# Modulation sums of a two-layer DiT trunk: VectorE folds the accumulators in turned 32x32 blocks, TensorE adds four partition groups with a selector

## The chip, the cores and the metric

The kernel runs on one core of a Trainium2 chip. The metric is device time in microseconds (us) of one execution. Five engines run in parallel, each through its own stream of instructions, and wait for one another by semaphores: TensorE (PE) multiplies 128x128 blocks and writes PSUM banks, VectorE (DVE) and ScalarE (ACT) work on elements, GpSimd (POOL) here mostly issues the DMAs of one weight matrix, SyncE (SP) issues the DMAs of all others.

## The reference, cut to what matters

Two layers of a trunk over 256 latent tokens (`x`) and 256 context tokens (`xc`), with 1024 channels, all in fp32. Each layer is FFN, mixers (attention and a short convolution), FFN, and every one of these is modulated by vectors made from a conditioning vector:

```python
c_act, cc_act = silu(c), silu(c_ctx)                # two vectors of 1024
mod  = (c_act  @ w_ada + b_ada).reshape(B, 9, 1, D) # w_ada: 1024 x 9216 in each layer
modc = (cc_act @ w_ada + b_ada).reshape(9, D)
x  = x  + 0.5 * mod[:, 2] * swiglu(modulate(rmsnorm(x, norm_w[0]), mod[:, 0], mod[:, 1]), ffn1_wi, ffn1_wo)
xc = xc + 0.5 * modc[2]   * swiglu(modulate(rmsnorm(xc, norm_w[0]), modc[0], modc[1]), ffn1_wi, ffn1_wo)
# mixers with mod 3, 4, 5; second FFN with mod 6, 7, 8
```

What the change touches is only `c_act @ w_ada` and `cc_act @ w_ada`: two rows times a 1024 x 1024 block of `w_ada` for each of 18 modulation vectors. All else is what stands beside it.

## The kernel before, in words

**Streamed weights.** Each large product takes 1024x1024-float pieces of weights through a ring of four slots (`raw`, `wH`, `wL`). SP loads `raw`; ACT copies it rounded to `wH` (`hi`, L1071); DVE makes the rest `wL = raw - wH` (`lo`, L1355); PE multiplies three times for every product (`triple`, L585 to L587), with the activations split in the same way. PE signals `w_used` behind each piece; a piece of 24 matmuls of 512 columns is one step of the ring. DVE signals `lo_done`, for which PE waits at the start of a piece. DVE makes the second pair of parts of a group of four pieces for the group that follows, so it is two pieces ahead.

**Modulation vectors.** The first two are made by PE at the very start (`ada_sums`, `ada_turn` with n < 4). The other 16 are spread over the kernel as five batches (`ADA_BATCHES`): 4, 2, 4, 2 and 4 vectors. Batches 0, 2 and 4 ("wi") run beside the first product of FFN 0, 1 and 2; batches 1 and 3 ("wo") beside the second product of FFN 0 and 1. POOL loads a 128x1024 row block of `w_ada` into one of four buffers; DVE multiplies it by a value per partition and adds it to the accumulator `acc` (`ada_tile`, L1399 for the first of eight blocks, L1402 for the other seven), twice, for `c` and for `c_ctx`. After eight blocks `acc[:, v, :]` (128 x 2 x 1024) still has to be summed over the 128 partitions.

**Sum over the partitions.** PE does it (`ada_reduce`, L611 to L619): four matmuls, one for each of the two vectors and two halves, with 4 columns of a one-hot matrix `oneh` as the stationary operand and 512 columns of `acc` moving. Each of the four writes another strip of 32 partitions of PSUM bank 5 (named `scored` in the trace), and the place of the one in `oneh` chooses the row of the vector within the strip. In the "wi" batches this stands in PE's order behind every second group of four pieces (four times in a batch), in the "wo" batches twice at once, in the opening of what follows (`ada_reduce_late`), when the new normed activations are being made. DVE may start the next accumulation in `acc` only when `ada_red` says that PE has read it.

**Rows to columns.** DVE copies bank 5 to `rowS` (`batch_rows`, L1378), PE turns it with four transposes (`ada_turn`, L607) into bank 6 (`turned`), and DVE adds the bias and writes `mod` (`batch_evac`, L1389). Bank 5 is set to zero by DVE before each use. In the "wi" batches PE's turn stands within group 9 of 11, in the "wo" batches within the opening.

**Order.** Each engine's order is written out by hand. PE's order in an FFN with a batch: the opening (pieces 0 to 3), groups 1 to 10, with `ada_reduce` after groups 2, 4, 6 and 8 and the turn inside group 9; then the second product. DVE's order in a group: `lo`, a block, `lo`, a block, two products (`product`, L1579 and L1587), `lo`, a block, `lo`, a block.

Of the kernel before, what the change touches and what calls it, by code (L numbers as in the profile page):

```python
# [7 lines left out]
P = 128  # L8
# [141 lines left out]
def build(nc, x, c, ctx, c_ctx, w_ada, b_ada, norm_w, ffn1_wi, ffn1_wo, w_in, conv_w, sink, w_oa, w_ob, w_out,  # L150
          ffn2_wi, ffn2_wo, final_norm_w, consts, out):
    stack = ExitStack()
    with stack:
# [34 lines left out]
        oneh = sb("oneh", [P, 16])  # L188
        sb("to_row", [P, 95])
        with ExitStack() as r:  # L190
# [5 lines left out]
            with ExitStack() as s:  # L196
                acc2 = s.enter_context(nc.sbuf_tensor("acc2", [P, 2, D], F32))

# [67 lines left out]
        ada_red = sem("ada_red")  # L266
        oneh_set = sem("oneh_set")
# [311 lines left out]
        def _(pe):  # L579
# [22 lines left out]
            def ada_turn(n):  # L602

                pe.wait_ge(row_out, n + 1)
                wait(pe, ada_out, n if n < QUARTERS else 2 * n - QUARTERS)
                for q in range(2 if n < QUARTERS else 4):
# [12 lines left out]

            def ada_reduce_late(b):  # L620

                pe.wait_ge(x_ready, x_count(b, DC - 1, 1))
                for u in range(2):
                    ada_reduce(acc[:] if u == 0 else acc2[:], 2 * DC * (ada_before(b) + u + 1), 3 - u, start=(u == 0))

            def opening(n0, v, ts, mids={}, between=None, ahead={}):
# [51 lines left out]
                for kk in (4, 6):  # L678
                    for j in (2, 3):
# [7 lines left out]
                        if kk == 6 and j == 2 and v in (1, 3):  # L687
                            ada_turn(QUARTERS + v)
# [146 lines left out]
            def ffn(f, v):  # L835
# [5 lines left out]
                def first_group():  # L841

                    if n0 > 0:
                        opening(n0, v, (t, t), second_norm(v) if halves(t) == 2 else {},
                                (lambda: ada_reduce_late(v)) if v == 3 else None)
# [5 lines left out]
                def group(i, turn=None):  # L851
# [3 lines left out]
                    for j in range(4):  # L855
# [3 lines left out]
                        if turn is not None and j == 1:  # L859
                            ada_turn(turn)  # L860
# [99 lines left out]
            def mixers(l):  # L960
# [4 lines left out]
                        (lambda: ada_reduce_late(v)) if v == 1 else None)  # L965
# [371 lines left out]
        def _(dve):  # L1337
# [36 lines left out]
            def batch_rows(b):  # L1374

                dve.wait_ge(ada_red, ada_before(b + 1))
                dve.wait_ge(ada_T, QUARTERS + b)
                nc.vector.tensor_copy(rowS[:], ps[5][:]).then_inc(row_out, 1)  # L1378

            def batch_evac(b):  # L1380

                _, _, first, count = ADA_BATCHES[b]
                dve.wait_ge(ada_T, QUARTERS + 1 + b)
                part = ps[6][:].rearrange("p (q v h u) -> p v u h q", q=4, v=2, h=2)
                at = V_BADA + DC * first
                bias = VT[:, at:at + DC * count].rearrange("p (u h q) -> p u h q", u=count, h=2)
                for v in range(2):
                    dst = mod[:, first:first + count, :, v].rearrange("p u (h q) -> p u h q", h=2)
                    tt(dst, part[:, v, 0:count], bias, ALU.add).then_inc(ada_out, 1)  # L1389

            def ada_tile(dst, src, n, reduced):
# [3 lines left out]
                if k == 0:  # L1395
                    wait(dve, ada_red, reduced)
# [475 lines left out]
```

## Time and profile before

| | us |
|---|---|
| median of 3 runs | 1832.9 (1832.73 to 1833.56) |
| profiled execution, span | 1832.8 |
| PE busy | 1818.3 (99%) |
| PE weight loads busy | 1543.2 (84%) |
| DVE busy | 1121.4 (61%) |
| ACT busy | 693.6 (38%) |
| POOL busy | 99.3 (5%) |

The profiled execution's own time is the span of 1832.8 us, 0.1 us from the median of the three timed runs. "Busy" of PE counts from the first to the last cycle of overlapping matmuls: a matmul of 512 columns has a record of 0.39 us, yet the next starts about 0.23 us after it.
### The profile page before, as it was taken

How to read it: one execution, taken by the hardware profiler on the slowest of the kernel's cores; microseconds unless marked ns; L12 is line 12 of the kernel's file. 1: busy time of each engine (PE TensorE's matmuls, PEld its weight loads, DVE VectorE, ACT ScalarE, POOL GpSimd, SP SyncE). 2: the span in 40 equal slices, each digit the busy share in tenths (PEclk: the TensorE clock that was granted, in tenths of full speed). 3: DMA queues.
4: the chain of work that ended last, by engine and by line, in shares of the span. 5: the costliest groups of instructions: out<-in, count | busy, mean ns of one | idle time of the engine just before them, and what ended most of it. 6: DMA issues, size and time to landing. Idle time of an engine off the chain costs nothing.

```text
span 1832.8 us, 26314 instructions
## 1 busy us (share of the span) xinstructions
PE 1818.3 (99%) x10131; PEld 1543.2 (84%) x10131; DVE 1121.4 (61%) x1506; ACT 693.6 (38%) x1093; POOL 99.3 (5%) x174
## 2 busy tenths in 40 slices
PE   9999999999999999999999999999999999999998
PEld 6888888888777789888888888888888888999998
DVE  5877737556554366877737557777422487676554
ACT  3433332244334324433332144333322365556543
POOL 0101001010000001000001010000000100000000
PEclk9999999999999999999999999999999999999999
DMA  9766526423222323666527435565222254546663
GB/s 335 227 189 189 155 92 232 146 70 102 74 78 70 92 80 127 185 191 188 159 92 229 149 115 172 176 196 169 92 94 101 69 150 139 150 143 202 195 195 115
DMA packets 187893, 271.49 MB, mean 148 GB/s; under 512 B 25388, under 2 KB 154908, under 8 KB 187804
## 3 DMA queue, kind: packets, MB, share of 16 engines
q1 hardware_dynamic: 168912, 202.74, 35.8%
q0 software_dynamic: 18432, 67.12, 12.0%
q8 instruction: 64, 1.05, 0.2%
q10 hardware_dynamic: 460, 0.39, 0.1%
q14 instruction: 25, 0.20, 0.0%
HBM read 269.16 MB, written 1.05 MB: 147 GB/s over the span
## 4 chain that ended last, share of the span: by engine, by line
PE 94%; DVE 3%; ACT 2%; issue 1%; DMA 0%; SPq 0%; ACTq 0%; DVEq 0%
PE ps L585 23%; PE ps L586 23%; PE ps L587 23%; PE turned L586 2%; PE turned L587 2%; PE turned L585 2%; PE scored L585 2%; PE scored L586 2%; PE scored L587 2%; PE ps L642 2%; PE ps L644 2%; PE ps L654 2%; PE turned L956 1%; PE turned L939 1%; PE scored L925 1%; PE scored L616 1%
## 5 line engine op out<-in xcount | busy, mean ns | idle before, releaser
L1355 DVE TENSOR_TENSOR wL<-raw,wH 128x1024 fp32r<-128x1024 f32 x364 | 443.3, 1223 | 447.4 <-ACT wH L1071 447.1
L1071 ACT ACTIVATE wH<-raw 128x1024 fp32r<-128x1024 f32 x364 | 383.1, 1057 | 663.8 <-PE ps L587 658.4
L585 PE MATMUL ps<-hH,wH 128*128 128x512 f32 (+1 forms) x1592 | 583.0, 366 | 0.6 <-ACT T L1164 0.6
L586 PE MATMUL ps<-hL,wH 128*128 128x512 f32 (+1 forms) x1592 | 578.5, 363 | 0.0
L587 PE MATMUL ps<-hH,wL 128*128 128x512 f32 (+1 forms) x1592 | 578.4, 363 | 0.0
L585 PEld LDWEIGHTS ps<-hH,wH 128*128 128x128 f32 x1592 | 299.0, 188 | 64.7 <-issue 16.3
L587 PEld LDWEIGHTS ps<-hH,wL 128*128 128x128 f32 x1592 | 298.9, 188 | 48.3
L586 PEld LDWEIGHTS ps<-hL,wH 128*128 128x128 f32 x1592 | 299.0, 188 | 46.5
L585 PE MATMUL ps<-GH,wH 128*128 (+2 forms) x376 | 131.5, 350 | 0.0
L587 PE MATMUL ps<-GH,wL 128*128 (+2 forms) x376 | 131.2, 349 | 0.0
L586 PE MATMUL ps<-GL,wH 128*128 (+2 forms) x376 | 131.2, 349 | 0.0
L1402 DVE SCALAR_TENSOR_TENSOR acc<-adaC,cact,acc 128x1024 f32<-128x1024 f32 x96 | 118.8, 1278 | 0.0
L1183 ACT ACTIVATE T<-ps 128x512 f32<-128x512 f32 (+1 forms) x88 | 43.1, 541 | 154.6 <-PE ps L587 148.9
L1171 ACT ACTIVATE GH<-T 128x512 f32 (+3 forms) x88 | 49.4, 579 | 114.1 <-DVE T L1579 114.1
L585 PEld LDWEIGHTS ps<-GH,wH 128*128 128x128 f32 x376 | 70.8, 188 | 9.5
L586 PEld LDWEIGHTS ps<-GL,wH 128*128 128x128 f32 x376 | 70.8, 188 | 9.3
L587 PEld LDWEIGHTS ps<-GH,wL 128*128 128x128 f32 x376 | 70.7, 188 | 9.3
L560 POOL TENSOR_TENSOR T<-T 128x256 f32<-128x256 f32 x30 | 22.9, 764 | 969.8 <-ACT T L1076 968.9
L1579 DVE TENSOR_TENSOR T<-T 128x512 f32<-128x512 f32 (+1 forms) x88 | 50.8, 619 | 31.2 <-ACT T L1164 31.2
L1402 DVE SCALAR_TENSOR_TENSOR acc<-adaW,cact,acc 128x1024 f32<-128x1024 f32 x56 | 69.3, 1278 | 0.0
L585 PE MATMUL ps<-nearH,wH 128*128 128x256 f32 x240 | 68.8, 287 | 0.0
L642 PE MATMUL ps<-hH,wH 128*128 128x256 f32 (+1 forms) x208 | 65.0, 332 | 2.8 <-ACT hH L1086 2.0
(249 smaller groups left out, 2509.4 us busy)
## 6 DMA issues: line engine op xcount, KB each, us to landing
raw<-in_ffn_wi SPq DMA_DIRECT2D x176, 512.0 KB, 3.9
raw<-in_ffn_wo SPq DMA_DIRECT2D x88, 512.0 KB, 3.4
raw<-in_w_in SPq DMA_DIRECT2D x60, 512.0 KB, 3.9
adaC<-in_w_ada POOLq DMA_DIRECT2D x48, 512.0 KB, 4.4
adaW<-in_w_ada POOLq DMA_DIRECT2D x32, 512.0 KB, 4.3
adaA<-in_w_ada POOLq DMA_DIRECT2D x24, 512.0 KB, 4.0
adaB<-in_w_ada POOLq DMA_DIRECT2D x24, 512.0 KB, 4.6
raw<-in_w_out SPq DMA_DIRECT2D x16, 512.0 KB, 3.3
```

Source lines behind the costliest of these rows:

```text
L585: mm(dst, wa, ra, start=start, stop=False, **kw)
L586: mm(dst, wa, rb, start=False, stop=False, **kw)
L587: return mm(dst, wb, ra, start=False, stop=stop, **kw)
L642: mm(ps[banks(j) + b][:, cols], wH[:, s, w], h_of(v)[0][:, kk, rows], start=(kk == 0 and cols.start == 0), stop=False, skip_group_check=True)
L644: mm(ps[banks(j) + b][:, cols], wL[:, s, w], h_of(v)[0][:, kk, rows], start=False, stop=False, skip_group_check=True)
L654: last = mm(ps[banks(j) + b][:, cols], wH[:, s, weights(j, kk % 4, b)], h_of(v)[1][:, kk, rows], start=False, stop=(kk == DC - 1), skip_gr ...
L1071: av(wH[:, s, :], raw[:, s, :], ACT.Copy).then_inc(hi_done, 1)
L1171: av(dst, T[:, 2 + b, 0:t], ACT.Copy).then_inc(g_hi, 1)
L1183: av(T[:, b, 0:t], ps[b][:, 0:t], ACT.Copy).then_inc(a_out, 1)
L1355: tt(wL[:, s, :], raw[:, s, :], wH[:, s, :].bitcast(F32), ALU.subtract).then_inc(lo_done, 1)
L1402: stt(dst[:, v, :], src, cact[:, v, k:k + 1], dst[:, v, :], ALU.mult, ALU.add).then_inc(acc_step, 1)
L1579: tt(T[:, 2 + b, 0:t], T[:, 2 + b, 0:t], T[:, b, 0:t], ALU.mult).then_inc(g_prod, 1)
```

## The change

The one-hot sums, the copy to rows and the transposes of the five batches go. Instead:

- DVE sums each accumulator itself over blocks (`fold`): one `tensor_reduce` over `acc` seen as 64 blocks of 32 columns, with `apply_transpose`, which turns each 32x32 block on the way in. What comes out is 128 x 64: in each group of 32 partitions, each partition holds the sum over the 32 partitions of its group, for one of every 32 columns. In "wi" batches it stands behind every second group and writes 64 columns of `rowS`; in "wo" batches it stands behind the block j = 8 (the first one of the second vector) and the block j = 15 and writes `late_sums`.
- PE adds the four groups of partitions (`ada_spread_out`): once in a batch, four matmuls with a 128x32 selector `sel` as the stationary operand and 64 (or 32, in "wo") columns of sums with a stride of four floats moving; each writes one strip of 32 partitions of bank 6. It stands where the turn stood in "wi" batches and where the late sums stood in "wo" batches.
- DVE adds the bias from bank 6 (`batch_evac`), with no copy to rows before. `ada_tile` waits for DVE's own `ada_folded` where it waited for PE.
- DVE makes `sel` once from the identity. `oneh` and the clearing of bank 5 between batches go.

```diff
-            def ada_reduce(src, steps, at, start=False):
-                pe.wait_ge(acc_step, steps)
-                for v in range(2):
-                    for h in range(2):
-                        g = 2 * v + h
-                        last = mm(ps[5][32 * g:32 * g + 4, :], oneh[:, at:at + 4],
-                                  src[:, v, h * TOK:(h + 1) * TOK], start=start, stop=True, skip_group_check=True)
-                last.then_inc(ada_red, 1)
-            def ada_reduce_late(b):
+            def ada_spread_out(b):
+                count = ADA_BATCHES[b][3]
+                sums = (rowS[:, 0:2 * D // 32 * count] if ADA_BATCHES[b][1] == "wi" else
+                        late_sums[:].rearrange("p u v c -> p (u v c)"))
+                pe.wait_ge(sel_set, 1)
+                pe.wait_ge(ada_folded, ada_before(b + 1))
+                pe.wait_ge(ada_out, QUARTERS + 2 * b)
+                for r in range(4):
+                    last = mm(ps[6][32 * r:32 * r + 32, 0:2 * DC * count], sel[:],
+                              sums.rearrange("p (n r) -> p n r", r=4)[:, :, r], start=True, stop=True, skip_group_check=True)
+                last.then_inc(ada_spread, 1)
+            def ada_late(b):
                 pe.wait_ge(x_ready, x_count(b, DC - 1, 1))
-                for u in range(2):
-                    ada_reduce(acc[:] if u == 0 else acc2[:], 2 * DC * (ada_before(b) + u + 1), 3 - u, start=(u == 0))
+                ada_spread_out(b)
...
-                        if kk == 6 and j == 2 and v in (1, 3):
-                            ada_turn(QUARTERS + v)
...
-                    pe.wait_ge(oneh_set, 1)
-                    pe.wait_ge(bank5_zero, f + 2)
-                    for p in range(4):
-                        group(2 * p + 1)
-                        group(2 * p + 2)
-                        ada_reduce(acc[:], 2 * DC * (ada_before(b) + p + 1), 3 - p, start=(p == 0))
-                    group(GROUPS - 2, QUARTERS + b)
+                    for i in range(1, GROUPS - 2):
+                        group(i)
+                    group(GROUPS - 2, b)
...
-            def batch_rows(b):
-                dve.wait_ge(ada_red, ada_before(b + 1))
-                dve.wait_ge(ada_T, QUARTERS + b)
-                nc.vector.tensor_copy(rowS[:], ps[5][:]).then_inc(row_out, 1)
...
-                dve.wait_ge(ada_T, QUARTERS + 1 + b)
+                dve.wait_ge(ada_spread, b + 1)
...
+            def fold(src, dst, n):
+                dve.wait_ge(acc_step, 2 * DC * (n + 1))
+                nc.vector.tensor_reduce(dst, src[:].rearrange("p v (c i) -> p (v c) i", i=32), AX_X, ALU.add,
+                                        apply_transpose=True).then_inc(ada_folded, 1)
...
-                    if hf == nh - 1 and m == 5 and v in (1, 3):
-                        batch_rows(v)
...
-                if v in (2, 3):
-                    nc.vector.memset(ps[5][:], 0.0).then_inc(bank5_zero, 1)
...
+                if f == 0:
+                    nc.vector.tensor_reduce(sel[:], ident.rearrange("p (r j) -> p j r", r=4), AX_X, ALU.add
+                                            ).then_inc(sel_set, 1)
...
                         group(2 * u + 2, DC * u + 4)
-                    batch_rows(b)
+                        fold(acc, rowS[:, 2 * D // 32 * u:2 * D // 32 * (u + 1)], ada_before(b) + u)
...
+                        if j in (DC, 2 * DC - 1):
+                            u = j // DC if j > DC else 0
+                            fold(acc2 if u else acc, late_sums[:, u].rearrange("p v c -> p (v c)"), ada_before(b) + u)
```

## Rows read from the trace of the kernel before

**Rows 1.** The page: busy time of the engines, and the chain that ended last.

```profile
PE 1818.3 (99%) x10131; PEld 1543.2 (84%) x10131; DVE 1121.4 (61%) x1506; ACT 693.6 (38%) x1093; POOL 99.3 (5%) x174
...
PE 94%; DVE 3%; ACT 2%; issue 1%; DMA 0%; SPq 0%; ACTq 0%; DVEq 0%
```

**Rows 2.** Timeline of PE, one sum: start, duration, what, count.

```profile
96.65 0.39 PE L587 MATMUL ps<-hH,wL 128*128 128x512 f32 x1
...
98.69 0.39 PE L587 MATMUL ps<-hH,wL 128*128 128x512 f32 x1
99.01 1.04 PE L616 MATMUL scored<-acc,oneh 128*4 128x512 f32 x8
99.98 0.50 PE L585 MATMUL ps<-hH,wH 128*128 128x512 f32 x1
100.32 0.39 PE L586 MATMUL ps<-hL,wH 128*128 128x512 f32 x1
```

**Rows 3.** The chain in order of time (start, duration): sums of "wi" batches.

```profile
99.08 0.97 PE scored L616 x8
143.80 0.97 PE scored L616 x8
...
1247.87 0.97 PE scored L616 x8
1292.63 0.97 PE scored L616 x8
```

**Rows 4.** Timeline of PE around the late sums of batch 1.

```profile
406.94 0.64 PE L654 MATMUL ps<-hL,wH 128*128 128x256 f32 x4
407.51 1.90 PE L616 MATMUL scored<-acc,oneh 128*4 128x512 f32 x16
409.34 0.38 PE L642 MATMUL ps<-hH,wH 128*128 128x256 f32 x1
409.56 0.28 PE L644 MATMUL ps<-hH,wL 128*128 128x256 f32 x1
```

**Rows 5.** Timeline of PE around the turn of batch 0.

```profile
244.99 0.40 PE L587 MATMUL ps<-hH,wL 128*128 128x512 f32 x1
245.22 0.60 PE L607 MATMUL turned<-cst,rowS 128*128 128x128 f32 x4
...
246.82 0.39 PE L587 MATMUL ps<-hH,wL 128*128 128x512 f32 x1
```

**Rows 6.** Timeline of PE around eight narrow records with full weights (mean squares).

```profile
394.93 0.28 PE L587 MATMUL ps<-GH,wL 128*128 128x256 f32 x1
395.05 0.51 PE L803 MATMUL scored<-cst,T 128*128 128x2 f32 x4
395.41 0.59 PE L803 MATMUL scored<-cst,sqT 128*128 128x2 f32 x4
...
396.06 0.28 PE L586 MATMUL ps<-GL,wH 128*128 128x256 f32 x1
```

**Rows 7.** Groups of weight loads by form: busy us, mean ns, idle before.

```profile
L803 PEld LDWEIGHTS scored<-cst,T 128*128 128x128 f32 x16 | 2.1, 192 | 0.0
...
L616 PEld LDWEIGHTS scored<-acc,oneh 128*4 128x4 f32 x128 | 2.0, 85 | 5.8 <-issue 5.5
```

**Rows 8.** Groups of DVE by form: a reduction over 1024 elements.

```profile
L1720 DVE TENSOR_REDUCE stat<-scored 128x2 f32<-128x1024 f32 x16 | 19.6, 1225 | 0.6
```

**Rows 9.** Timeline of DVE where the first fold will stand; idle before in brackets.

```profile
90.47 2.48 DVE L1402 SCALAR_TENSOR_TENSOR acc<-adaC,cact,acc 128x1024 f32<-128x1024 f32 x2
95.74 1.23 DVE L1355 TENSOR_TENSOR wL<-raw,wH 128x1024 fp32r<-128x1024 f32 x1 [2.79 <-ACT wH L1071]
100.19 1.42 DVE L1399 TENSOR_SCALAR acc<-adaA,cact 128x1024 f32<-128x1024 f32 x2 [3.23 <-PE scored L616]
```

**Rows 10.** Busy time in one stretch from sum to sum: length, PE, PEld, DVE, ACT, POOL, PE clock.

```profile
99.00:143.70 44.70, 44.70 (x201) 36.08 (x200) 32.88 (x32) 14.61 (x20) 4.22 (x8) 1.00 0.63 188
```

**Rows 11.** Waits: total us, times, longest.

```profile
DVE acc L1399 <- PE scored L616: 29.1, 9, 3.2
DVE rowS L1378 <- PE scored L616: 21.5, 3, 7.2
```

**Rows 12.** Timeline of DVE in the second product of FFN 0.

```profile
318.85 1.41 DVE L1399 TENSOR_SCALAR acc<-adaW,cact 128x1024 f32<-128x1024 f32 x2
323.15 1.23 DVE L1355 TENSOR_TENSOR wL<-raw,wH 128x1024 fp32r<-128x1024 f32 x1 [2.89 <-ACT wH L1071]
```

**Rows 13.** Timeline of the opening after the late sums: ACT's h parts, then PE.

```profile
414.10 0.51 ACT L1086 ACTIVATE hH<-T,mod 128x256 fp32r<-128x256 f32 x1 [1.41 <-DVE T L1427]
```

**Rows 14.** The same opening, PE's first matmul of chunk 5.

```profile
416.58 0.39 PE L642 MATMUL ps<-hH,wH 128*128 128x512 f32 x1
```

More of the change, by code:

```diff
@@ L186, in build @@
         stat = sb("stat", [P, 6, 4])
-        oneh = sb("oneh", [P, 16])
-        sb("to_row", [P, 95])
+        sel = sb("sel", [P, P // 4])
+        sb("to_row", [P, 79])
         with ExitStack() as r:
@@ L265, in build @@
         acc_step = sem("acc_step")
-        ada_red = sem("ada_red")
-        oneh_set = sem("oneh_set")
+        ada_folded = sem("ada_folded")
+        ada_spread = sem("ada_spread")
+        sel_set = sem("sel_set")
         ada_out = sem("ada_out")
@@ L604, in ada_turn @@
                 pe.wait_ge(row_out, n + 1)
-                wait(pe, ada_out, n if n < QUARTERS else 2 * n - QUARTERS)
-                for q in range(2 if n < QUARTERS else 4):
+                wait(pe, ada_out, n)
+                for q in range(2):
                     last = nc.tensor.transpose(ps[6][:, q * P:(q + 1) * P], rowS[:, q * P:(q + 1) * P], ident)
                 last.then_inc(ada_T, 1)
-            def ada_reduce(src, steps, at, start=False):
-                pe.wait_ge(acc_step, steps)
-                for v in range(2):
-                    for h in range(2):
-                        g = 2 * v + h
-                        last = mm(ps[5][32 * g:32 * g + 4, :], oneh[:, at:at + 4],
-                                  src[:, v, h * TOK:(h + 1) * TOK], start=start, stop=True, skip_group_check=True)
-                last.then_inc(ada_red, 1)
-            def ada_reduce_late(b):
+            def ada_spread_out(b):
[10 more added lines that the diff above has]
+            def ada_late(b):
                 pe.wait_ge(x_ready, x_count(b, DC - 1, 1))
-                for u in range(2):
-                    ada_reduce(acc[:] if u == 0 else acc2[:], 2 * DC * (ada_before(b) + u + 1), 3 - u, start=(u == 0))
+                ada_spread_out(b)
             def opening(n0, v, ts, mids={}, between=None, ahead={}):
@@ L844, in first_group @@
                         opening(n0, v, (t, t), second_norm(v) if halves(t) == 2 else {},
-                                (lambda: ada_reduce_late(v)) if v == 3 else None)
+                                (lambda: ada_late(v)) if v == 3 else None)
                         return
@@ L849, in first_group, with group @@
                             None, {1: lambda: ada_sums(1), 3: lambda: ada_sums(2), 5: lambda: ada_sums(3)})
-                def group(i, turn=None):
+                def group(i, batch=None):
                     pe.wait_ge(a_out, i * 2 + 2 * GROUPS * f)
@@ L858, in group @@
                         columns_piece(n0, j, 2 * (j % 2), j // 2, t, i, span(t))
-                        if turn is not None and j == 1:
-                            ada_turn(turn)
+                        if batch is not None and j == 1:
+                            ada_spread_out(batch)
                 b = ada_batch(f, "wi")
@@ L964, in mixers @@
                 opening(n0, v, (TOK, t), second_norm(v),
-                        (lambda: ada_reduce_late(v)) if v == 1 else None)
+                        (lambda: ada_late(v)) if v == 1 else None)
                 for h in range(4, PROJ_P):
@@ L1372, in ada_evac, with ada_tile @@
                 tt(dst, part[:, :, :, 1, 0:2], dst, ALU.add).then_inc(ada_out, 1)
[L1374 to L1378 removed]
             def batch_evac(b):
                 _, _, first, count = ADA_BATCHES[b]
[L1383 to L1384 removed]
+                dve.wait_ge(ada_spread, b + 1)
+                part = ps[6][:, 0:2 * DC * count].rearrange("p (u v k) -> p v u k", u=count, v=2)
                 at = V_BADA + DC * first
[L1386 removed]
+                bias = VT[:, at:at + DC * count].rearrange("p (u k) -> p u k", u=count)
                 for v in range(2):
[L1388 to L1391 removed]
+                    tt(mod[:, first:first + count, :, v], part[:, v], bias, ALU.add).then_inc(ada_out, 1)
+            def ada_tile(dst, src, n, folded):
                 k = n % DC
@@ L1395, in ada_tile @@
                 if k == 0:
-                    wait(dve, ada_red, reduced)
+                    wait(dve, ada_folded, folded)
                 for v in range(2):
@@ L1829, in _ @@
             nc.vector.memset(ps[5][:], 0.0).then_inc(bank5_zero, 1)
-            mark(nc.vector.memset(oneh[:], 0.0))
-            settle()
-            nc.vector.memset(oneh[:, 3:4], 1.0).then_inc(oneh_set, 1)
             for hf in range(2):
```

2 lines of the change are left out of this document (1 added, 1 removed).

## The prediction

> **What bounds the kernel now.** I read the page first: PE is busy for 1818.3 of 1832.8 us, and 94% of the chain that ended last is PE's [rows 1]. So a PE instruction that goes away is time won, as long as nobody else becomes late; DVE, at 61%, has room on average, and the question is whether it has room where the new work is put. Then I looked for the instructions that go in the chain in order of time: the "wi" sums stand on it, 0.97 us each, three of four shown in pairs 44.7 us apart [rows 3]. To price them I went to PE's timeline around each kind, because matmul records overlap and only the distance between starts is a cost.
>
> **The cadence.** From 96.65 to 98.69 there are nine steps: 2.04 / 9 = 0.2267 us for a matmul of 512 columns [rows 2]. Half width goes at 0.12 us.
>
> **Removed from PE.** (a) *Twelve "wi" sums.* Between the starts of two of them lie eight pieces of 24 matmuls: 143.80 - 99.08 = 44.72 us, and 1292.63 - 1247.87 = 44.76 [rows 3]; 192 x 0.2267 is 43.52. One sum therefore costs 1.20 us, refilling the pipeline included. The direct view agrees: L586 starts at 100.32 where the cadence would have put it at 98.69 + 0.45 = 99.14, so 1.18 [rows 2]. 12 x 1.20 = 14.4 us. (b) *Two pairs of late sums.* The four L654 from 406.94 end their steps at 407.42, the L644 after the next would start at 407.54 and starts at 409.56: 2.02 us [rows 4]. 2 x 2.02 = 4.0. (c) *Five turns.* From 244.99 to 246.82 are six steps, 1.36 us by the cadence, and it took 1.83: 0.47 us [rows 5]. 5 x 0.47 = 2.4. Together 20.8 us, all in PE's order and with PE busy on both sides.
>
> **Added to PE: five spreads.** The trace has no 128x32 stationary operand, so I bound it. One sum costs 1.20, two in a row 2.02: the second, eight records of 512 columns in four strips, costs 0.82, and entering and leaving costs 0.38. The spread is eight records in the same four strips with 64 columns (three batches) or 32 (two): 0.82 x 64 / 512 = 0.10 or 0.05. That gives the lower bound, 0.48 and 0.43 us: 2.3 us for the five. What it leaves out is the weights: 32 columns to load where the sum loads 4. A load of 4 columns has a record of 85 ns, one of 128 columns 192 ns [rows 7], so 32 columns come at some 109 ns, 24 ns more, 0.19 us for eight if nothing of it is hidden. The upper bound is eight narrow records with full weights, the mean squares: 396.06 - 394.93 less two steps of 0.12 is 0.89 us [rows 6]; with the 0.38 on top it would be 1.27, or 6.4 us for the five. I take the row that it is nearest to (same strips, narrow weights), with half the extra load hidden: 0.58 and 0.53, so 3 x 0.58 + 2 x 0.53 = 2.8 us. The moving operand with a stride of four floats I cost at nothing: 64 columns are too few for a doubled read to cost over 0.1 us each.
> The 0.38 us that a run of strip-wise matmuls pays however short it is has a rule beside it: the Trainium skill, "TensorEngine Tiling (Array Packing)", Key Properties, says that a change of the tiling mode drains TensorE. It speaks against hoping for a free spread; by that rule the change keeps 5 of 14 drains, and the trace agrees, since the second sum of a pair does not pay it again.
>
> **Net on PE:** 20.8 - 2.8 = 18.0 us.
>
> **Added to DVE: sixteen folds.** A reduction of 1024 elements takes 1.225 us [rows 8], of 2048 some 2.3 to 2.45 us if the turning costs nothing. I take 2.4 us, and bound it below by 2.2 and above by nothing in the trace, since no row has a turned input; so I ask what cover there is. In "wi" batches the fold stands behind the last block, which ends at 92.95, and ahead of a `lo` that began at 95.74 because ACT's part was not ready: DVE stood idle for 2.79 us just there, and for 3.23 us more, two instructions later, for PE's sum [rows 9]. The second wait is gone, for the next block now waits for the fold itself. So a fold of up to 2.8 us delays nobody, and one of up to 6.0 us lets the block after it start no later than today. From sum to sum DVE is busy for 32.88 of 44.70 us [rows 10]; the stretch shrinks to 43.5, which leaves 10.6 us for one fold. PE needs that `lo` only 11 us later (it is for the third piece of the next group). What is queued behind the fold on DVE is `lo`, the product and, through `acc_step`, POOL's next loads; all keep today's time. The waits that vanish, 29.1 us over nine blocks and 21.5 us over three copies [rows 11], were not on PE's path, so they are worth nothing by themselves. In "wo" batches DVE has 2.89 us idle right where the first fold stands [rows 12], and the second, at j = 15, has the same room and no block behind it. Nothing is costed here.
>
> **Late spread and the opening.** In the opening the late sums also gave ACT and DVE time to make the activations. With 2.02 - 0.53 = 1.5 us taken out, PE asks for chunk 5 of the second half at 416.58 - 1.5 = 415.1 [rows 14]; ACT's part of it ended at 414.10 + 0.51 = 414.6 [rows 13]. That is the tightest of the eight, by 0.5 us, and by the order of instructions the 0.6 us copy to rows stood behind it, so its going does not help there. The cover holds, barely; if it did not, up to 0.5 us for each of two openings would come back.
>
> **Small things, costed at nothing.** The copies to rows, the clearings of bank 5 and `oneh` leave DVE where it waits for others; the selector is one small reduction behind the first `lo`s, where DVE then waits again. `batch_evac` of a late batch no longer waits for the turn, and its reader comes later. POOL's and SP's queues keep their order; no DMA is added.
>
> **Sum.** 1832.8 - 18.0 = 1814.8 for the span; the median of the runs stands 0.1 above the profiled span: **1814.9 us**.
>
> **Rivals.**
> *The spread is dear.* Narrow matmuls go one behind another with full load times. For it: the mean squares cost 0.89 us for eight records, though they move two columns only [rows 6]. Against: there the weights are 128 columns wide. It gives 1832.9 - 20.8 + 6.4 = 1818.5.
> *A late fold holds up PE's operands in places.* If a turned element costs three times a plain one, a fold is 7.3 us: still below 10.6, but beyond the 6.0 us of idle time next to it, so the following product and ACT's copy come up to 1.3 us later, and the opening and the "wo" pieces (1.8 to 2.9 us idle a piece) are pressed at the two late folds. I price that at 3 us in all: about 1818.
> *Slower: DVE becomes the bound.* The place is the stretch from fold to fold in "wi" batches. It decides from 10.6 us for one fold, which is 5.2 ns an element against the 1.2 ns of the row; the kernel as a whole is slower once 12 x (fold - 10.6) exceeds 18, so from 12.1 us. A block of 32x32 that is filled and drained with nothing overlapping, and each with several passes for four-byte elements, might be six times the plain 2.4: 14.4 us, 12 x 3.8 = 46 us lost, 1814.9 + 46 = 1861.
> The Trainium skill, "VectorE: DVE Perf Modes", Rules for kernel authors, speaks against this change: it advises to keep `tensor_reduce` off a hot path, as the slowest of DVE's operations at one element a cycle. The trace agrees on the rate (1.225 us for 1024 elements), but DVE's path is not the hot one here, so by that rule too the time is 1814.9.
> *It does nothing.* If PE ran into a wait that the sums now hide everywhere, it would stay at 1832.9. Against it: PE's order is one unbroken run on both sides of the sums, at the same cadence.
>
> **Chances.** Forecast, all cover holds and the spread is below 0.8 us: 0.84 (1814.2 to 1816.5). Dear spread 0.07, late fold 0.04, nothing 0.02, slower 0.03. The range that holds 8 in 10 and takes in the bounds of the spread: the lower one, 20.8 - 2.3 = 18.5, gives 1814.4, and rounding of the starts (0.05 us at each of 19 places) another 1 below it: 1813.4; upwards to the dear spread: 1818.8. A measurement of this kernel can tell some 0.2%, 3.7 us, from no change. Faster by more than that: 0.84 + 0.07 + 0.04 = 0.95; within: 0.02; slower: 0.03.
>
> **What would show it.** PE's starts in groups 1 to 8 at one cadence with no gap from 55 to 233 us; in group 9 a gap of 0.5 to 0.7 us with x8 records of 64 columns; stretches of two groups at 43.5 instead of 44.7 us; the end of FFN 0 about 5 us earlier. A fold record of 2.3 to 2.5 us, followed by a shorter wait for ACT. In the opening no PE wait above 0.3 us on ACT's h part. Wrong would be: folds above 6 us, PE waiting for `wL` of L1355, or a spread whose strips don't overlap.

## The result, and the profile after

The changed kernel took 1815.75 us in the median of four runs (1814.14 to 1817.2) against 1833.08 for the kernel before. The ratio on record, from the repeated executions, is 0.9892 with a 95% interval of 0.9872 to 0.9912; the plain quotient of the two medians is 0.9905, inside that interval. On another chip the ratio was 0.9892 again (0.9876 to 0.9909), with medians of 1815.75 and 1834.25 us. The forecast was 1814.9 us in a range of 1813.4 to 1818.8. The median lies in it; the ratio, put on the 1832.9 us of before, gives 1813.1, just below its lower end. Some executions of either kernel take 5 to 7 us longer than the rest (in the traces that caught one, in a stage at the end that the change does not touch), so the small differences below are read from starts of instructions and not from times.

The page after: busy time of the engines, and the chain by engine.

```profile
PE 1799.6 (99%) x10023; PEld 1540.2 (85%) x10023; DVE 1154.5 (64%) x1513; ACT 693.7 (38%) x1093; POOL 99.4 (5%) x174
...
PE 93%; DVE 4%; ACT 2%; issue 1%; DMA 0%; SPq 0%; ACTq 0%; DVEq 0%
```

PE is busy for 18.7 us less than in [rows 1], the span is 18.8 us shorter (1814.0), and DVE is busy for 33 us more. PE bounds it as before.

The timeline of PE where a spread replaced the turn of batch 0, which [rows 5] show (start, duration, what, count):

```profile
239.80 0.39 PE L589 MATMUL ps<-hH,wL 128*128 128x512 f32 x1
240.12 0.42 PE L621 MATMUL turned<-rowS,sel 128*32 128x64 f32 x8
240.47 0.50 PE L587 MATMUL ps<-hH,wH 128*128 128x512 f32 x1
240.80 0.40 PE L588 MATMUL ps<-hL,wH 128*128 128x512 f32 x1
```

The timeline of DVE at the place of [rows 9], with the idle time before in brackets:

```profile
92.66 2.31 DVE L1398 TRANSPOSE_TENSOR_REDUCE rowS<-acc 128x64 f32<-128x2048 f32 x1
95.41 1.22 DVE L1353 TENSOR_TENSOR wL<-raw,wH 128x1024 fp32r<-128x1024 f32 x1 [0.45 <-ACT wH L1069]
96.56 1.41 DVE L1390 TENSOR_SCALAR acc<-adaA,cact 128x1024 f32<-128x1024 f32 x2
99.94 1.23 DVE L1353 TENSOR_TENSOR wL<-raw,wH 128x1024 fp32r<-128x1024 f32 x1 [1.98 <-ACT wH L1069]
```

The fold took 2.31 us and filled the gap: of the 2.79 us of idle time ahead of the `lo`, 0.45 are left, and the 3.23 us for PE's sum are gone. The block of the next vector now starts at 96.56, 3.6 us earlier than the 100.19 of [rows 9] (0.3 us of that was won before this point, see below).

**Where the time went, start by start.** TensorE's matmuls with streamed weights (those that read `wH` or `wL`) are the same 9096 records in the same order in all 14 traces, so the n-th of one can be set against the n-th of another. The difference of the starts, before less after, then grows where something was taken out.

```
before: start us   difference   step
            23.9        -0.02
            41.02        0.32    +0.34  opening of FFN 0
            96.65        0.33    +0.01
           102.38        1.52    +1.19  sum 1 of batch 0
           148.94        2.75    +1.23  sum 2
           193.24        3.98    +1.23  sum 3
           237.51        5.19    +1.20  sum 4
           251.59        5.07    -0.11  spread in place of the turn
           410.39        6.68    +1.60  late spread in place of two sums (batch 1)
           429.77        7.15    +0.47  turn of batch 1
           942.89       11.84    +4.84 for the four sums of batch 2, -0.13 for its spread
          1099.01       13.45    +1.61  batch 3
          1117.22       13.94    +0.50  turn of batch 3
          1296.62       18.81    +4.87  four sums of batch 4
          1311.82       18.68    -0.13  spread of batch 4
          1822.14       18.68     0.00
```

All steps but the first stand at the places that the change names. Between them the difference doesn't move by more than 0.1 us up to the last FFN, and by 0.25 us in it.

The first step was forecast by nothing. It sits in the opening of FFN 0. The timelines of DVE and of PE there, the kernel before and then the changed one:

```profile
39.05 0.16 DVE L1562 SCALAR_TENSOR_TENSOR normA<-mod,VT 128x4 f32<-128x4 f32 x1
39.54 0.48 DVE L1427 SCALAR_TENSOR_TENSOR T<-X,normA,scored 128x256 f32<-128x256 f32 x1 [0.33 <-DVE normA L1562]
41.02 0.50 PE L642 MATMUL ps<-hH,wH 128*128 128x512 f32 x1 [0.72 <-ACT hH L1086]
```

```profile
39.02 0.16 DVE L1554 SCALAR_TENSOR_TENSOR normA<-mod,VT 128x4 f32<-128x4 f32 x1
39.22 0.48 DVE L1424 SCALAR_TENSOR_TENSOR T<-X,normA,scored 128x256 f32<-128x256 f32 x1
40.70 0.50 PE L646 MATMUL ps<-hH,wH 128*128 128x512 f32 x1 [0.42 <-ACT hH L1084]
```

In the kernel before, DVE stands still for 0.33 us in front of an instruction that the change does not touch; ACT's `hH` and PE's wait for it follow. The trace of the kernel before and that of its variant with one strip have this gap, and none of the twelve traces of the changed kernel and its variants has it. So the 0.3 us come with the change. Which part of the edit removes them was not tried: all that differs in DVE's source ahead of this point is that `oneh` is no longer made.

### The profile page after: what moved, and what is told of

Its sections match the earlier page's. It is cut to its first block, busy times and chain, and to the rows that moved or that the text cites. A ratio compares the mean times of both kernels' runs of the same rounds, so it can differ in the third digit from the quotient of the medians.

```text
span 1814.0 us, 26097 instructions
## 1 busy us (share of the span) xinstructions
PE 1799.6 (99%) x10023; PEld 1540.2 (85%) x10023; DVE 1154.5 (64%) x1513; ACT 693.7 (38%) x1093; POOL 99.4 (5%) x174
## 4 chain that ended last, share of the span: by engine, by line
PE 93%; DVE 4%; ACT 2%; issue 1%; DMA 0%; SPq 0%; ACTq 0%; DVEq 0%
PE ps L587 23%; PE ps L589 23%; PE ps L588 23%; PE turned L589 2%; PE turned L587 2%; PE turned L588 2%; PE scored L587 2%; PE scored L589 2%; PE scored L588 2%; PE ps L646 2%; PE ps L648 2%; PE ps L658 2%; PE turned L954 1%; PE turned L937 1%; PE scored L923 1%
```

## The experiments

**The changed kernel again.**

> The changed kernel as it is, beside the kernel before on the same chip, to learn what a timed run holds outside its span and whether the 0.3 us that the first 40 us gained belong to the change. Theory (the gain is all on TensorE: 14.6 us of sums, 3.2 of late sums, 0.6 of turns less spreads): span 18.3 to 18.7 us below that of before, median 17.5 to 18.7 below. Rival (part of the gain is lost outside the span, since the first four timed runs gave only 17.3): the time outside the span is larger by 0.5 us or more than that of before, in every run.

The timed runs gave 0.9892 of before, median 1815.75 against 1834.25, so 18.5 us below it. Here the executions of both kernels lasted 2.0 to 2.2 us longer than their spans: before 1830.6 to 1832.8 of span for 1832.8 to 1834.8 of time, but for one of 1839.15. In the other runs it is 2.0 to 2.2 us for the kernel before and mostly 2.0 to 2.3 for the changed kernel and its variants, with ten executions between 2.4 and 3.2, one of them among the first four timed runs. So a span of 1832.8, as the profiled execution of before had it, goes with a time some 2 us above the median, and no run loses 0.5 us outside the span in every execution. The rival falls. The first step of the table is not there between this trace and the first one of the changed kernel: their difference is 0.12 us at the first large matmul and 0.12 to 0.16 us from there to 1430 us. Two traces of one kernel part by more in three places: where the first large matmul starts (22.3 to 24.3 us over all traces), by up to 1.5 us between 1440 and 1620 us, and in the last FFN. Busy time in two stretches of the last FFN, first of the changed kernel, then of the same kernel again (length, PE with its records, PEld, DVE, ACT, POOL, granted clock, DMA share, GB/s):

```profile
1650.00:1700.00 50.00, 50.00 (x444) 50.00 (x443) 29.59 (x39) 27.16 (x46) 0.00 (x0) 1.00 0.63 195
```

```profile
1650.00:1700.00 50.00, 50.00 (x427) 50.00 (x426) 28.44 (x37) 26.71 (x44) 0.00 (x0) 1.00 0.59 182
```

The same stretch held 444 and 427 matmuls, 0.1133 and 0.1178 us from start to start, with a granted clock of 1.00 in both and PE never waiting. Over 1440 matmuls of that FFN it is 163.2 against 169.6 us, 6.4 us.

**Without the spreads.**

```diff
-                for r in range(4):
-                    last = mm(ps[6][32 * r:32 * r + 32, 0:2 * DC * count], sel[:],
-                              sums.rearrange("p (n r) -> p n r", r=4)[:, :, r], start=True, stop=True, skip_group_check=True)
-                last.then_inc(ada_spread, 1)
...
-                dve.wait_ge(ada_spread, b + 1)
```

> The five spreads and the wait of VectorE for them are left out, the folds stay; the modulation vectors then hold what bank 6 held before, so the output is not the reference's. Theory (a spread costs 0.59 us in the wi batches, as the turn that it replaced plus 0.11, and 0.43 in the late ones): 3 x 0.59 + 2 x 0.43 = 2.6 us below the changed kernel, with a step of just this size at each place. Rival (a spread is dearer in all than the starts around it show, since the cadence after it is slower for a while): 4 us or more. Rival (its wait is what costs): the steps stay within 0.1 us of today's.

The steps against the changed kernel were 0.59 us at each of the three "wi" places, and 0.23 at each of the late ones: 2.2 us, where 2.6 was expected, with 1813.6 us in the median. The "wi" price holds to the hundredth. The late one does not, though the starts around the late spread show 0.43. The timelines of PE there say why, first of the changed kernel, then of this one:

```profile
401.86 0.64 PE L658 MATMUL ps<-hL,wH 128*128 128x256 f32 x4
402.43 0.30 PE L621 MATMUL turned<-late_sums,sel 128*32 128x32 f32 x8
402.67 0.39 PE L646 MATMUL ps<-hH,wH 128*128 128x256 f32 x1
402.89 0.28 PE L648 MATMUL ps<-hH,wL 128*128 128x256 f32 x1
```

```profile
401.47 0.64 PE L654 MATMUL ps<-hL,wH 128*128 128x256 f32 x4
402.06 0.36 PE L642 MATMUL ps<-hH,wH 128*128 128x256 f32 x1
402.25 0.28 PE L644 MATMUL ps<-hH,wL 128*128 128x256 f32 x1
```

The four from 401.47 end their steps at 401.95, yet the L644 that was due at 402.07 starts at 402.25. ACT makes the first part of the second half (`hH`, chunk 0) at just that time:

```profile
401.41 0.91 ACT L1080 ACTIVATE hH<-T,mod 128x256 fp32r<-128x256 f32 x2 [2.68 <-DVE T L1419]
```

Two of them in 0.91 us: the first is there at about 401.9. So PE seems to arrive in step with its operand, and 0.2 us of the spread's 0.43 to stand in for that wait. That the break is this wait and not the bare cost of the semaphore waits at the seam was not separated.

**Without folds and spreads.**

```diff
-                nc.vector.tensor_reduce(dst, src[:].rearrange("p v (c i) -> p (v c) i", i=32), AX_X, ALU.add,
-                                        apply_transpose=True).then_inc(ada_folded, 1)
+                return
```

> Spreads and folds both left out: no sum over the partitions is made by any engine, the output is not the reference's. Beside the run with folds and no spreads it prices the 16 folds (2.3 us each on VectorE, 37 us in all). Theory (they hide wholly behind VectorE's waits for ScalarE): within 0.1 us of the run without spreads when the starts of TensorE are compared one by one, and within noise in the time. Rival (a fold disturbs TensorE or ScalarE by its traffic in SBUF, or delays a late operand): 0.5 us or more below it, in steps at the 16 places.

From 96 to 237 us, over four folds of batch 0, the difference to the changed kernel stayed at 1.65 us, and over those of the other "wi" batches at 2.45 and 3.24, without a step of 0.01 us (the 1.65 us were there at the first large matmul). The steps at the three spreads were 0.59. A fold does not move TensorE by 0.01 us. Median 1813.57 against 1813.63 without spreads alone.

**Full-width spreads.**

```diff
-                    last = mm(ps[6][32 * r:32 * r + 32, 0:2 * DC * count], sel[:],
+                    last = mm(ps[6][:, 0:2 * DC * count], ident,
```

> Each spread is made with the 128x128 identity as the stationary operand, writing all 128 partitions of bank 6 four times, in place of the 128x32 selector in four strips; the same moving operand. The output is not the reference's. Theory (what a strip-wise run pays at its ends, 0.38 us, belongs to the change into strips, and full weights cost about 0.1 us a record): 8 records at 0.11 less the 0.38 that goes: 0.8 to 0.9 us a spread in wi batches, 0.2 to 0.4 above today's; 1 to 1.5 us in all above the changed kernel. Rival (the 0.38 us is the price of any break in the run of large matmuls, strips or not): 1.2 to 1.3 us a spread, 3.3 us in all.

0.34 us more than today's at each of the three "wi" places: 0.93 us a spread; 0.49 and 0.47 more at the late ones. That is 2.0 us in all, above the 1 to 1.5 that the theory gave and below the rival's 3.3. At the "wi" places the rival's 1.2 to 1.3 us a spread is excluded, so there the 0.38 us is not on top. Eight full-width records cost what the mean squares of [rows 6] cost, 0.89, whatever they move. The Trainium skill, "TensorEngine Tiling (Array Packing)", Key Properties, has TensorE drain when the tiling mode changes, and these don't change it; the number agrees with that rule, but no run here changes the mode and nothing else, so that the drain is the 0.38 us is argued, not shown.

**Longer folds.** Every fold made four, six and eight times.

```diff
+                for _ in range(3):  # 5 and 7 in the others
+                    mark(nc.vector.tensor_reduce(dst, src[:].rearrange("p v (c i) -> p (v c) i", i=32), AX_X, ALU.add,
+                                                 apply_transpose=True))
+                    settle()
```

> Each of the 16 folds is made four times, one behind the other with a wait between, the same result: some 9.4 us on VectorE in place of 2.3. Theory (a fold is free up to the idle time of VectorE from fold to fold): VectorE is busy 35.2 of 43.5 us now, 42.3 with this, so still within: the time of the changed kernel within 1 us, and TensorE's starts in groups 1 to 8 at one cadence. Rival (late fold: what counts is the 6 us of idle time next to the fold, and the products behind it come late): 3 us or more above the changed kernel.

> Each fold made six times, some 14.1 us. VectorE then needs 47.0 us for a stretch that TensorE does in 43.5. By the prediction's price for the slower rival, 12 x 3.5 = 42 us above the changed kernel, so 1858. Other theory: VectorE's lead over TensorE, some 10 us at the start of a batch, is used up first, 3.5 us a stretch, and only what is over stops TensorE: 4 x 3.5 - 10 = 4 us a batch, 12 in all and a few at the late folds, so 1828 to 1832.

> Each fold made eight times, some 18.8 us; VectorE needs 51.7 us a stretch, 8.2 over. Prediction's price: 12 x 8.2 = 98 us above the changed kernel. With the lead used up first: 3 x (33 - 10) = 69, and 10 to 15 at the late folds of the second product: 1895 to 1900. Both say slower than before: the point of decision, 18 us lost, lies below this one.

Busy time in a stretch of 44 us of batch 0, first of x4, then of x6 and x8 (these two at a later stretch than x4's):

```profile
98.00:142.00 44.00, 44.00 (x196) 36.44 (x195) 42.20 (x37) 14.52 (x20) 4.22 (x8) 1.00 0.62 191
```

```profile
186.00:230.00 44.00, 40.55 (x173) 33.15 (x172) 42.93 (x36) 12.25 (x17) 2.64 (x5) 0.96 0.49 153
```

```profile
186.00:230.00 44.00, 38.76 (x160) 31.52 (x160) 42.83 (x34) 12.36 (x17) 3.16 (x6) 0.92 0.46 140
```

With four, DVE is busy for 42.20 of 44 us and PE for all of them: 1815.97 us, and TensorE's starts stay within 0.08 us of the changed kernel's up to 1480 us. A fold of 9.3 us is free, in the late places too. With six, PE stands still, and the granted clock of the stretch falls from 1.00 to 0.96 (with eight to 0.92). PE's largest wait in x6 and in x8, in all, times, longest:

```profile
PE ps L587 <- DVE wL L1353: 16.7, 9, 3.5
```

```profile
PE ps L587 <- DVE wL L1353: 47.4, 12, 8.2
```

x6 took 1844.4 us, 1.0059 of before (1.0043 to 1.0074): slower by a little, where the prediction's price said 1858 and the other theory 1828 to 1832. In starts it lost 9.2, 9.3 and 9.3 us in the three "wi" batches, 27.8 in all, and nothing in "wo". The single steps (batch 0: 2.3, 5.2 and 1.7 us; batch 4: 3.9, 3.8 and 1.6) show the mechanism: DVE is late by 3.5 us a stretch, its lead covers the first of them, and then TensorE pays. Taken from the totals the lead is 4 x 3.5 - 9.3 = 4.7 us, not the 10 that the other theory took, and not zero as in the prediction's formula.

But not all that is lost is waiting. PE in x6 behind its longest wait, where the granted clock from 201 to 204 us was 0.50, the level of 1.2 GHz:

```profile
201.09 0.80 PE L587 MATMUL ps<-hH,wH 128*128 128x512 f32 x1 [3.45 <-DVE wL L1353]
201.68 0.63 PE L588 MATMUL ps<-hL,wH 128*128 128x512 f32 x1
202.11 0.63 PE L589 MATMUL ps<-hH,wL 128*128 128x512 f32 x1
...
204.24 0.40 PE L588 MATMUL ps<-hL,wH 128*128 128x512 f32 x1
204.47 0.40 PE L589 MATMUL ps<-hH,wL 128*128 128x512 f32 x1
```

The matmuls behind this wait start 0.43 us apart for a while instead of 0.23. In the three batches PE stood idle for 7.0, 6.1 and 5.4 us, and such slow starts cost another 1.6, 2.6 and 3.1 us. So the 4.7 us lump two things that happen to offset each other: the last stretch is not paid in full (1.6 us of waiting at the spread of batch 0), and the clock adds to the waits.

x8 took 1927.7 us, 1.0507 (1.0478 to 1.0537): 30.1, 29.8 and 29.5 us in the "wi" batches, where 33 less 4.7 would be 28, and 9.5 and 9.3 us at the pairs of late folds. The expectation said 1895 to 1900, the prediction's formula 1913: both too low. Slow starts are 9.4, 9.5 and 5.6 us of what the three batches lost, and neither had a term for them.

**One strip instead of four.** On the kernel before.

```diff
-                for v in range(2):
-                    for h in range(2):
+                for v in range(1):
+                    for h in range(1):
```

> The kernel before with one of the four matmuls of each partition sum (the first vector's first half), the other three left out; the output is not the reference's. It tells what a sum on TensorE is paid for. Theory (the four strips run at once, and what is paid is the 512 moving columns of one, 0.82 us, and 0.38 at the ends): a sum still costs 1.1 to 1.2 us and the time stays within 1 us of before. Rival (the four matmuls run one behind the other, each a quarter of 0.82): 0.6 us a sum, 9.8 us less for the 16.

The chain in order of time, where [rows 3] have 0.97 us for eight records:

```profile
144.22 0.95 PE scored L616 x2
188.94 0.95 PE scored L616 x2
```

The ratio to before is 1.0008 (0.9995 to 1.0021), and the starts gain 0.02 to 0.04 us a "wi" sum. Three of four matmuls are free: a sum was paid for 512 moving columns and its ends.

**Five spreads in a row, with and without the stride.**

```diff
-                for r in range(4):
-                    last = mm(ps[6][32 * r:32 * r + 32, 0:2 * DC * count], sel[:],
-                              sums.rearrange("p (n r) -> p n r", r=4)[:, :, r], start=True, stop=True, skip_group_check=True)
+                for r in range(20):
+                    last = mm(ps[6][32 * (r % 4):32 * (r % 4) + 32, 0:2 * DC * count], sel[:],
+                              sums.rearrange("p (n r) -> p n r", r=4)[:, :, r % 4], start=True, stop=True, skip_group_check=True)
```

> Each spread is issued five times in a row, 20 matmuls of 128x32 in four strips in place of 4, the same result. It splits a spread's 0.59 us (64 columns) into what is paid once and what each set of eight records costs. Theory (0.38 us at the ends, the rest per set): a further set costs 0.10 to 0.21 us, so 0.4 to 0.8 us more at each wi place, 1.5 to 3 us in all. Rival (weights of a strip are not loaded beside the other strips' streaming): 0.109 us a record, 8 records 0.87 us, so 3.5 us more a place and 17 us in all.

0.91 us more at "wi" places: four further sets at 0.23 each, a little above the theory's 0.10 to 0.21 and far below the rival's 0.87; at the late ones 0.12 a set. Half the columns, half the price: it is the columns, at twice the rate of the sum's. So the next run took away the stride.

```diff
-                              sums.rearrange("p (n r) -> p n r", r=4)[:, :, r % 4], start=True, stop=True, skip_group_check=True)
+                              sums.rearrange("p (r n) -> p r n", r=4)[:, r % 4], start=True, stop=True, skip_group_check=True)
...
-                nc.vector.tensor_reduce(dst, src[:].rearrange("p v (c i) -> p (v c) i", i=32), AX_X, ALU.add,
+                nc.vector.tensor_reduce(dst, src[:].rearrange("p v (m r i) -> p (v m) r i", r=4, i=32), AX_X, ALU.add,
```

Both calls of `fold` hand over their part of the destination in the new order. The kernel is otherwise that of the run before.

> The run with each spread five times over, with one thing changed: VectorE writes the folded sums with the four groups r apart, so that the moving operand of a spread is 64 (or 32) columns next to each other in place of a stride of four floats. The result is the same. With the stride a further set of eight records cost 0.23 us with 64 columns and some 0.12 with 32. Theory (the stride halves the rate at which the moving operand is read; the prediction costed it at nothing): 0.10 to 0.12 us a further set of 64 columns and 0.05 to 0.06 of 32, so four sets take 0.4 to 0.5 us at a wi place. Rival (it is the loading of 32 columns of weights, which the prediction allowed 0.19 us for): no change, 0.91 us at a wi place.

Timelines of PE at the spreads of batch 0, first with the stride, then without:

```profile
238.66 1.35 PE L621 MATMUL turned<-rowS,sel 128*32 128x64 f32 x40
239.94 0.50 PE L587 MATMUL ps<-hH,wH 128*128 128x512 f32 x1
```

```profile
238.88 0.77 PE L621 MATMUL turned<-rowS,sel 128*32 128x64 f32 x40
239.57 0.50 PE L587 MATMUL ps<-hH,wH 128*128 128x512 f32 x1
```

The same 40 records took 1.28 us to the next large matmul with the stride and 0.69 without, and five contiguous sets cost 0.33 us more than today's single one, at each of the three places: 0.92 us, or 0.11 a further set. The theory holds there, the rival falls. At the late places five sets of 32 contiguous columns cost 0.27 us more than today's one; with the 0.31 us that the strided sets left for the break that makes some 0.08 a set (an estimate), where 0.05 to 0.06 was expected. So the stride is dear there too, but with 32 columns something beside the columns counts. After the fact, a rule bears on it: the Trainium skill, "SBUF — State Buffer", Door 1 (the note on cachelines), says that accesses want two hits in a 16-byte line for full bandwidth; four floats apart is one hit a line, and the doubled price per column agrees. The same note gives "4 fp32" as how far one can stride for free. Read as a step of four floats, that is not so here: the measured 0.23 against 0.11 us decides.

**The late spreads at another place, and both edits together.**

```diff
-                return {(0, 1, "within"): lambda: mean_squares(v, 1), (0, 2, "within"): lambda: spread_roots(v, 1)}
+                def squares_and_spread():
+                    mean_squares(v, 1)
+                    if v in (1, 3):
+                        ada_late(v)
+                return {(0, 1, "within"): squares_and_spread, (0, 2, "within"): lambda: spread_roots(v, 1)}
...
-                        (lambda: ada_late(v)) if v == 1 else None)
```

> The changed kernel with the two late spreads moved from between the halves of the opening to right behind the second mean squares in it, where TensorE's run of large matmuls is broken anyway; the result is the same. Theory (a break of its own costs a spread some 0.2 us of its 0.43, and between the halves 0.2 us of the 0.43 covered a wait for ScalarE's first part of the second half, which shows when the spread is left out): the spread costs about 0.3 us at the new place and 0 to 0.2 us of wait stays between the halves: 0 to 0.3 us less in all two places. Rival (the wait between the halves comes back in full and the break is not shared): 0.2 to 0.5 us more.

-0.33 and +0.50 us in the first opening, -0.32 and +0.50 in the second: 0.17 and 0.18 less, 0.35 in all, just above the theory's 0 to 0.3. At the seam between the halves nothing is left to pay (PE's timeline):

```profile
402.21 0.64 PE L658 MATMUL ps<-hL,wH 128*128 128x256 f32 x4
402.69 0.28 PE L646 MATMUL ps<-hH,wH 128*128 128x256 f32 x1
402.81 0.28 PE L648 MATMUL ps<-hH,wL 128*128 128x256 f32 x1
```

PE comes there later than in the run without spreads, and the break of 0.2 us is gone. That agrees with a wait for ACT, but the semaphore waits of the spread moved away too, so it doesn't settle it. The timed median, 1818.6 us, does not resolve so little.

> The changed kernel with the late spreads behind the mean squares (0.17 us less at each of the two places in the run before) and with contiguous moving operands. The result is the same. Theory: 0.11 us less at each of three wi places and 0.05 at the late ones on top, so 0.7 to 0.8 us below the changed kernel in TensorE's starts; in the timed runs within noise of it. Rival (the weights set the price): 0.34 us below. A strided write by VectorE might slow the fold; it has room for four times its length.

A single contiguous spread, the timeline of PE:

```profile
240.04 0.39 PE L589 MATMUL ps<-hH,wL 128*128 128x512 f32 x1
240.36 0.32 PE L621 MATMUL turned<-rowS,sel 128*32 128x64 f32 x8
240.61 0.50 PE L587 MATMUL ps<-hH,wH 128*128 128x512 f32 x1
240.94 0.39 PE L588 MATMUL ps<-hL,wH 128*128 128x512 f32 x1
```

At the "wi" places it gained 0.11, 0.11 and 0.12 us, and from 96 to 1293 us 0.73 in all, as expected. The fold with a strided result took 2.315 us, so nothing more. Timed, it is not told from the changed kernel: 0.9896 of before (0.9871 to 0.9922), lowest 1813.40 against 1814.14, median 1820.2 against 1815.75, and the kernel before on that chip at 1835.7. It beats before; that it beats the changed kernel is shown in starts only.

## Why the prediction was right or wrong, point by point

The mechanism was right: TensorE bounds the kernel, the work came off its path, and nobody became late. What failed is a size, in the step "Net on PE: 20.8 - 2.8 = 18.0 us". In starts the net is 18.7 us, more than the 18.5 that the prediction reached with its lowest price of a spread. The largest missing term, 0.33 us, lies in the opening of FFN 0; the prediction had no term for it and put what it called small things at nothing. The next, 0.23 us, is the late places, mis-sized by 0.11 and 0.12 us. Put through the ratio, the gain is 19.8 us (1832.9 to 1813.1); of this the starts place 18.7, and where the rest would lie no run shows (the interval of the ratio is 1809.4 to 1816.8 us).

- **What bounds it, and the removed work: right.** Twelve sums were priced at 14.4 us and gave 14.56 (1.19 to 1.24 each); the late turns, priced at 0.94, gave 0.97. That matmuls go for their moving columns, four strips for one, was implied by the price taken from starts, and the run with one strip shows it.
- **The price of a "wi" spread: right in size, wrong in its reason.** 0.58 us was forecast and 0.59 measured. But the 0.10 above the lower bound was put to the loading of 32 columns of weights, half hidden, and the stride was "costed at nothing". It is the other way round: with contiguous columns the spread costs 0.59 - 0.11 = 0.48, the lower bound itself, so the weights are hidden and the stride is all of it. Two errors of the same size cancelled, and that the price came out is luck. The 0.1 us that the text named as the most that a doubled read could cost is what it did cost (0.11), three times, and it was no reason to put it at nothing.
- **The late places: mis-sized.** Forecast 2.02 - 0.53 = 1.49 us, measured 1.60 and 1.61. The spread of 32 columns costs 0.43 in starts, again the lower bound.
- **The cover in the opening: named at the wrong chunk.** The step took chunk 5 as the tightest, by 0.5 us. By the run without spreads it was chunk 0 of the second half, where PE arrives as ACT finishes (argued from the starts, as said there); the step looked at the chunks after the sums and not at the very first, which had 2 us of sums ahead of it. With the spread in place it holds, without it 0.2 us of wait appear. It cost nothing here.
- **The folds: right.** 2.4 us forecast, 2.31 measured, no cost on TensorE to 0.01 us. The turning of the blocks is free, which no row of before had shown. That the idle time next to a fold is its cover was wrong, see the late fold below.
- **The sum.** 18.0 us was forecast for the span and 18.7 came: 0.33 of the difference is the step in the opening of FFN 0, 0.23 the late places, 0.16 the price of the sums.
- **How the profiled execution stands to the median: wrong.** The step set the span of 1832.8 against the median of 1832.9 and took 0.1 us as what lies around it. Around it lie some 2.1 us, so the execution was about 2 us longer than the median. It did no harm, because a difference was added to it.
- **The rivals.** *Dear spread:* 0.93 us with full weights is the worst that was tried, 2.0 us for the five above today's, not 3.6. (The sum for this rival is 1818.5; the upper end of the range, 1818.8, is 0.3 above it without a reason given.) *Late fold:* its threshold, 6.0 us, is wrong: 9.3 us are free. The idle time next to an instruction bounds nothing where the engine has a lead; what decides is the stretch. *Slower:* right in its mechanism and in the sign at 14.1 us; its bound of 10.6 us a stretch fits (9.3 is free, 14.1 is not), its price left out the lead and the lower clock behind a wait. With 4.7 us for the two together, 3 x (4 x (fold - 10.6) - 4.7) reaches the 18.7 us gained at 13.3 us; the prediction said 12.1. No run lies between 9.3 and 14.1, so this is an estimate. *It does nothing:* fell.

## What to carry to other kernels

Price work on the bounding engine from the distance between starts before and behind it, once alone and once twice in a row: that splits it into what a break costs (0.37 us here) and what the columns cost, and both carried over to an operation that the trace did not have. Work moved to an engine that runs ahead is free until the busy time of a whole stretch passes the length of the stretch; local idle time understates that, and beyond it the lead pays for the first part only, while TensorE's clock adds to the price of each long wait. For a small matmul, lay the moving operand out contiguously: here the engine that writes it did so at no cost.

## What the runs showed of the hardware that was not expected

- A `tensor_reduce` on VectorE that turns 32x32 blocks on the way in took 2.31 us for 128x2048 fp32, 1.13 ns an element, against 1.225 us for 1024 elements without (those from PSUM, these from SBUF): the turning adds nothing.
- Four matmuls in four strips of 32 output partitions cost what one costs: 0.97 against 0.95 us on the chain for 512 fp32 columns, and the loads of 32 columns of weights (records of 108 ns, eight of them) are hidden too.
- A moving operand with a stride of four floats costs twice as much per column: 0.23 against 0.11 us for a set of eight records of 64 columns.
- Behind TensorE's wait of 3.45 us in the run with six folds the next six matmuls of 512 columns started 0.43 us apart instead of 0.23 (granted clock 0.50), and behind one of 6.5 us with eight folds the next thirteen, so a wait costs more than its length. Behind a wait of 1.97 us the clock stayed up; behind one of 2.01 us in a later batch it did not.
- The last FFN of the kernel (256 columns a matmul) runs through at 0.1133 or at 0.1178 us from start to start, in both cases with a granted clock of 1.00 and no wait: 5 of 14 traces had the longer one. What decides it stays open; no run tried it.
